# Expert products with the tokens stationary and the weights moving, half rows gathered and scattered, and the down products one expert behind

## The chip, the core and the metric

One core of one Trainium2 chip runs the whole program. The metric is device time in microseconds (us) from launch to end, the median of repeated runs. The core has five engines with a queue each: TensorE (PE; its weight loads are shown apart as PEld), VectorE (DVE), ScalarE (ACT), GpSimd (POOL) and SyncE (SP). Each runs its own list of instructions in order and waits at semaphores for the others. Matrix products read the on-chip memory (SBUF, 128 partitions) and write PSUM, of which each of eight banks holds 128 partitions of 512 floats. DMA engines move data between SBUF and the chip's large memory (HBM).

## The reference

The program is one layer of a decoder over 512 tokens of width 1024: a mixing part (windowed attention, convolution, a matrix memory), then a mixture of experts, then an input embedding. The change is in the mixture. Each token is routed to 2 of 32 experts, so an expert gets 32 tokens in the mean. An expert computes, on its tokens' normed rows:

```
def run_block(args):
    idx, e, w = args
    xb = x_pad[idx]
    hb = jax.nn.silu(xb @ w_gate[e]) * (xb @ w_up[e])
    return (hb @ w_down[e]) * w[:, None]
```

(width 1024 to 256 twice, and back to 1024), and the weighted results are added to the tokens' rows. All of it is in float32.

## The kernel before

**Blocks and table.** An expert has room for BLK = 64 tokens. Tokens beyond 64 would go to overflow blocks, which run only if a count isn't zero; with these inputs none runs. VectorE works out for each of the 1024 (token, choice) pairs its slot, GpSimd scatters 8 x 128 records of four 32-bit words (token, result row, weight, 0) into `table_dram` (L1540), SyncE reads the table back to SBUF with one DMA (L499): slot j in partition j, one column for each block.

**One expert n.** GpSimd gathers its 64 rows of 4 KB from `normed` in HBM into `xr[n % 2]` by an indirect DMA (`gather`, L1557). TensorE turns them, 8 blocks of 64x128, into the bank TR (`turn_block`, L1004), VectorE multiplies by the norm's gain into `xT` (`turned_block`, L1430). `up` (L1013, recorded as L735, the line of the helper `mm`): for each of four 128-wide pieces of the hidden layer (two of gate, two of up) 8 products over the width, with the **weights stationary** (128x128) and the **tokens moving** (64 columns). ScalarE takes the sigmoid (L690), VectorE makes two products (L1438, L1441) that give `hx`, hidden width on partitions. `down` (L1026): four products, tokens stationary (128x64) and 512 columns of the down weights moving. ScalarE scales the low half of the result by the token's weight (L693), VectorE the high half (L1446), into `yr`. GpSimd scatters the 64 rows of 4 KB to `expert_rows` in HBM (`scatter`, L1566).

**What sets the order.** The lists are written by hand. TensorE, for each n: up(n), turn_block(n+1), down(n). GpSimd, for each n: gather(n+2), once block n is turned; then scatter(n), once both halves of expert n's result are scaled. Two small operations (L1549) carry waits ahead of each indirect DMA. SyncE keeps a ring of RING = 4 experts' weights in SBUF (`we`, 3072 KB an expert); the load of expert n+4 (L474) is issued when down(n) is done, and waits for nothing else. After expert 29 and 30 two loads of 2048 KB for the next stage take the place of expert loads (L509).

Ahead of the stage TensorE multiplies the input embedding and ends that before the table is ready. Behind it SyncE reads all of `expert_rows` once the last scatter has landed.

A product of float32 appears in the trace as two records, each a weight load (LDWEIGHTS, PEld) and a pass (MATMUL, PE). "PE bank L735 128*64 128x512" is a pass with 128 rows and 64 columns of weights and 512 moving columns.

## Time and profile before

| | |
|---|---|
| median of 3 runs | 1278.75 us (1278.14 to 1278.79) |
| profiled execution, span of the engines' work | 1272.7 us |
| PE busy | 1173.6 us (92%) |
| PEld busy | 849.9 us (67%) |
| DVE, ACT, POOL busy | 461.0, 288.0, 204.6 us |
| HBM read | 172.06 MB |

The profiled execution has no launch time of its own beside its span; the runs' median is 6.05 us above it, which is what lies around the engines' work. Times in the trace count from the start of the span. The expert stage runs from 801 to 1185 us. A granted clock of 1.00 means that TensorE runs at 2.4 GHz, 0.50 means 1.2 GHz.

### The profile page before, as it was taken

Reading aid. Unit: us, or ns where it says so; the run is one execution under the profiler, and the core shown is the slowest. Engines: PE = TensorE matmul, PEld = TensorE weight load, DVE = VectorE, ACT = ScalarE, POOL = GpSimd, SP = SyncE. Lnnn points to the kernel's source line nnn. Section 1 sums busy time; section 2 is a strip of 40 time slices with the busy share of each in tenths; the row PEclk is TensorE's granted clock in tenths of the full one; section 3 lists DMA queues with packets and bytes.
Section 4 is the critical chain, followed back from the end, with each engine's and each line's share of the span. In section 5 each row is a group of like instructions: output and inputs, shape, how many; then the busy total and the mean of one; then the engine's idle time right before and its main releaser. Section 6 shows DMA issues by size and latency. Waiting matters only on the chain.

```text
span 1272.7 us, 15378 instructions
## 1 busy us (share of the span) xinstructions
PE 1173.6 (92%) x5677; PEld 849.9 (67%) x5677; DVE 461.0 (36%) x981; ACT 288.0 (23%) x449; POOL 204.6 (16%) x384
## 2 busy tenths in 40 slices
PE   6699899899999889999999997799999999999596
PEld 6578678677677656666665464678777877777342
DVE  5594384476457336222321234011111111111433
ACT  2224333433422333111110111010110110110142
POOL 0222401501321110000000002122222222222000
PEclk9899899899899879999999987599999999999798
DMA  4220041031030214221214333178777777774401
GB/s 185 83 83 18 3 146 33 1 132 49 0 115 0 75 74 199 82 75 74 80 68 167 131 139 142 43 294 314 284 275 307 303 275 285 313 289 179 156 17 49
DMA packets 23133, 176.20 MB, mean 138 GB/s; under 512 B 5856, under 2 KB 6336, under 8 KB 16832
## 3 DMA queue, kind: packets, MB, share of 16 engines
q1 hardware_dynamic: 17504, 167.35, 34.4%
q0 software_dynamic: 5600, 8.47, 1.9%
q8 instruction: 18, 0.29, 0.1%
q14 instruction: 11, 0.09, 0.0%
HBM read 172.06 MB, written 12.65 MB: 145 GB/s over the span
## 4 chain that ended last, share of the span: by engine, by line
PE 80%; DVE 8%; issue 6%; DMA 2%; ACT 2%; POOL 1%; DVEq 0%; SPq 0%; ACTq 0%; POOLq 0%
PE bank L735 76%; DVE arena L1199 2%; PE bank L1004 2%; DVE low_parts L1132 2%; DVE arena L1239 1%; DMA arena<-in_w_branch 1%; PE bank L955 1%; PE bank L827 0%; DVE hT_parts L1127 0%; DMA x_sb<-in_x 0%; PE bank L763 0%; POOL table_dram L1540 0%; DMA arena<-expert_rows 0%; ACT arena L605 0%; DMA mT<-normed,gidx 0%
## 5 line engine op out<-in xcount | busy, mean ns | idle before, releaser
L735 PE MATMUL bank<-yT,arena 128*128 128x64 f32 (+1 forms) x2240 | 328.3, 307 | 0.9 <-DVE yT L1430 0.9
L735 PEld LDWEIGHTS bank<-yT,arena 128*128 128x128 f32 x2240 | 274.0, 196 | 63.0 <-issue 60.1
L735 PE MATMUL bank<-arena 128*128 128x64 f32 (+7 forms) x624 | 187.4, 452 | 23.1 <-DVE arena L1223 8.9
L735 PE MATMUL bank<-mT_parts,low_parts 128*128 128x512 f32 x448 | 178.7, 399 | 0.0
L735 PEld LDWEIGHTS bank<-arena 128*128 128x128 f32 (+1 forms) x624 | 108.7, 215 | 97.9 <-issue 70.6
L735 PE MATMUL bank<-mT_parts,x_parts 128*128 128x512 f32 x320 | 139.9, 437 | 17.3 <-DVE low_parts L1132 13.5
L735 PE MATMUL bank<-hT_parts,x_parts 128*128 128x512 f32 x320 | 128.4, 401 | 0.0
L735 PE MATMUL bank<-arena,yT 128*64 128x512 f32 x256 | 118.0, 604 | 0.0
L1132 DVE TENSOR_TENSOR low_parts<-arena,x_parts 128x1024 fp32r<-128x1024 f32 (+1 forms) x44 | 62.3, 1416 | 149.2 <-ACT x_parts L559 117.9
L735 PEld LDWEIGHTS bank<-mT_parts,low_parts 128*128 128x128 f32 x448 | 85.6, 191 | 20.9
L735 PEld LDWEIGHTS bank<-mT_parts,x_parts 128*128 128x128 f32 x320 | 61.8, 193 | 38.8 <-issue 18.8
L1199 DVE SCALAR_TENSOR_TENSOR arena<-arena,chn 128x512 f32<-128x512 f32 x116 | 80.5, 761 | 0.0
L735 PEld LDWEIGHTS bank<-hT_parts,x_parts 128*128 128x128 f32 x320 | 61.9, 193 | 19.0 <-issue 5.7
L735 PE MATMUL bank<-arena,hT 128*128 128x512 f32 (+1 forms) x192 | 72.3, 530 | 0.8 <-DVE hT L1091 0.8
L735 PEld LDWEIGHTS bank<-arena,yT 128*64 128x64 f32 x256 | 32.7, 138 | 59.3 <-issue 57.1
L693 ACT ACTIVATE mT<-bank,table 64x512 f32<-64x512 f32 x32 | 21.8, 682 | 200.8 <-PE bank L735 200.8
L1549 POOL TENSOR_TENSOR takes_wait<-cst 1x1 f32<-1x1 f32 x132 | 24.1, 183 | 264.5 <-issue 253.3
L1239 DVE CUSTOM_DVE_ANT_0 arena<-bank,arena 128x128 f32<-128x128 f32 (+3 forms) x96 | 38.7, 454 | 72.4 <-issue 59.9
L735 PEld LDWEIGHTS bank<-arena,hT 128*128 128x128 f32 x192 | 39.1, 244 | 31.7 <-issue 30.6
L1446 DVE TENSOR_SCALAR mT<-bank,table 64x512 f32<-64x512 f32 x32 | 23.8, 743 | 99.5 <-PE bank L735 99.5
L735 PE MATMUL bank<-mT_parts,cm_high_b 128*128 128x512 f32 x128 | 51.0, 398 | 3.5 <-DVE low_parts L1132 3.5
L1527 POOL TENSOR_TENSOR arena<-arena 128x128 f32<-128x128 f32 (+3 forms) x32 | 31.7, 992 | 124.3 <-ACT arena L605 124.3
(225 smaller groups left out, 1190.1 us busy)
## 6 DMA issues: line engine op xcount, KB each, us to landing
arena<-in_w_expert SPq DMA_DIRECT2D x32, 3072.0 KB, 10.6
arena<-in_w_cm SPq DMA_DIRECT2D x32, 512.0 KB, 3.5
arena<-in_w_gate SPq DMA_DIRECT2D x8, 1536.0 KB, 6.4
arena<-in_w_tm SPq DMA_DIRECT2D x4, 1536.0 KB, 6.8
arena<-in_w_branch SPq DMA_DIRECT2D x8, 768.0 KB, 7.9
x_sb<-in_x SPq DMA_DIRECT2D x8, 512.0 KB, 5.7
arena<-in_w_out SPq DMA_DIRECT2D x1, 4096.0 KB, 12.1
arena<-in_w_pg SPq DMA_DIRECT2D x2, 2048.0 KB, 7.7
```

Source lines behind the costliest of these rows:

```text
L693: act.activation(yr[b2][:, 0:512], OUT[0:BLK, :], ACT.Copy, scale=table_w(col)).then_inc(y_low, 1)
L735: return pe.matmul(out, lhsT, rhs, start=start, stop=stop)
L955: last = pe.transpose((S_16, OUT)[half][:, k * P:(k + 1) * P], x_sb[:, t, (4 * half + k) * P:(4 * half + k + 1) * P], ident)
L1004: last = (pe.matmul if k == 0 else pe.transpose)(TR[:, k * BLK:(k + 1) * BLK], xr[b2][:, k * P:(k + 1) * P], ident[0:BLK, 0:BLK], **(dict( ...
L1132: dve.tensor_tensor(low, weights, high.bitcast(F32), ALU.subtract).then_inc(done, 1)
L1199: dve.scalar_tensor_tensor(cacc[:, j % 2], ypad[:, j:j + SEQ], w31(j), cacc[:, j % 2], ALU.mult, ALU.add).then_inc(conv_step, 1)
L1239: dve.tensor_tensor_reduce(out=sc[:, u % 2, at:at + width], in0=bank[:, 0:width], in1=bias[:, s, b0:b0 + width], scale=1.0, scalar=-3e38, ...
L1446: dve.tensor_scalar(yr[b2][:, 512:1024], S_16[0:BLK, :], table_w(col), None, ALU.mult).then_inc(y_high, 1)
L1527: pool.tensor_tensor(dst[:, 0:n], sc[:, u % 2, 0:n], sc[:, u % 2, n:2 * n], ALU.add).then_inc(pool_step, 1)
L1549: pool.tensor_tensor(takes_wait[:, cell:cell + 1], ones[0:1, 0:1], ones[0:1, 0:1], ALU.add)
```

## The change

Up: the tokens become stationary (128x64) and the weights move. The hidden layer's 512 columns are cut in two sides of 256 (gate piece and up piece of one half); side 0 is multiplied in array columns 0 to 63 with its result in partitions 0 to 63 of a bank, side 1 in array columns 64 to 127 with its result in partitions 64 to 127. Down does the same with two sides of 512 columns in one bank. The hidden block now has tokens on partitions, so TensorE turns it (one 128x128) and ScalarE copies it back. The rows are gathered and scattered as 128 half rows of 2 KB; the table holds a record for each half. TensorE's list puts down(n) behind up(n+1). Banks for up (GU), down (Y) and the small tiles are doubled.

```
-        xr = [mflat[0:BLK, b * D:(b + 1) * D] for b in range(2)]
-        yr = [mflat[0:BLK, (2 + b) * D:(3 + b) * D] for b in range(2)]
+        xr = [mflat[:, b * 512:(b + 1) * 512] for b in range(2)]
+        yr = [mflat[:, (2 + b) * 512:(3 + b) * 512] for b in range(2)]
+        normed_halves = normed.rearrange("s (h c) -> (s h) c", h=2)
+        expert_halves = expert_rows.rearrange("s (h c) -> (s h) c", h=2)
+        GU, HT, Y = (MM, S_1), S_4, (OUT, S_16)
...
-            sp.dma_start(table[:, :, :], table_dram.rearrange("(j b) w -> j b w", b=NBLK)).then_inc(table_loaded, 16)
+            for half in range(2):
+                sp.dma_start(table[half * BLK:(half + 1) * BLK, :, :],
+                             table_dram.rearrange("(j b) w -> j b w", b=NBLK)[:, :, 4 * half:4 * half + 4])\
+                  .then_inc(table_loaded, 16)
...
-            def expert(n, b2, col, first_wait):
-
-                act.wait_ge(g_done, n + 1)
-                act.activation(sgx, MM[:, 0:2 * BLK], ACT.Sigmoid).then_inc(gate_sig, 1)
-                act.wait_ge(down_done, 2 * n + 1)
-                first_wait()
-                act.activation(yr[b2][:, 0:512], OUT[0:BLK, :], ACT.Copy,
-                               scale=table_w(col)).then_inc(y_low, 1)
+            def hidden_copy(n, b2):
+
+                act.wait_ge(h_turned, n + 1)
+                act.activation(hx[b2], HT[:, 0:P].rearrange("p (j s) -> p j s", j=2), ACT.Copy).then_inc(hx_ready, 1)
+
+            def scale_rows(n, b2, scattered):
+
+                act.wait_ge(down_done, n + 1)
+                act.wait_ge(rows_scattered[b2], scattered)
+                act.activation(yr[b2], Y[b2][:, :], ACT.Copy, scale=table_w(n)).then_inc(y_scaled, 1)
...
+                for k in range(KD // 2):
+                    last = pe.transpose(TR[:, k * P:(k + 1) * P], xr[b2][:, k * P:(k + 1) * P], ident)
+                last.then_inc(rows_turned, 1)
+
+            def up(n, b2, w, gu_free):
+
+                pe.wait_ge(xT_ready, n + 1)
+                gu_free()
                 for k in range(KD):
-
-                    last = (pe.matmul if k == 0 else pe.transpose)(
-                        TR[:, k * BLK:(k + 1) * BLK], xr[b2][:, k * P:(k + 1) * P], ident[0:BLK, 0:BLK],
-                        **(dict(start=True, stop=True) if k == 0 else {}))
-                last.then_inc(rows_turned, 1)
-
-            def up(n, b2, w):
-
-                for m in range(4):
-                    for k in range(KD):
-                        last = mm((MM, S_1)[m // 2][:, m % 2 * BLK:(m % 2 + 1) * BLK],
-                                  w[:, k * 512 + m * P:k * 512 + (m + 1) * P],
-                                  xT[b2][:, k, :], k == 0, k == KD - 1)
-                    if m % 2:
-                        last.then_inc((g_done, u_done)[m // 2], 1)
-
-            def down(n, w):
+                    for side in range(2):
+                        last = mm(GU[b2][side * BLK:(side + 1) * BLK, 0:2 * P], xT[b2][:, k % 4, k // 4, :],
+                                  w[:, k * 512 + side * 2 * P:k * 512 + (side + 1) * 2 * P], k == 0, k == KD - 1)
+                last.then_inc(up_done, 1)
+
+            def turn_hidden(n, b2):
+
+                pe.wait_ge(h_swished, n + 1)
+                pe.transpose(HT[:, 0:P], hs[b2], ident).then_inc(h_turned, 1)
+
+            def down(n, b2, w, y_free):
+
                 pe.wait_ge(hx_ready, n + 1)
-                pe.wait_ge(y_low, FREE + n)
-                pe.wait_ge(y_high, FREE + n)
-                for half in range(2):
-                    for j in range(2):
-                        at = 4096 + j * 1024 + half * 512
-                        last = mm((OUT, S_16)[half][0:BLK, :], hx[:, j, :], w[:, at:at + 512], j == 0, j == 1)
-                    last.then_inc(down_done, 1)
+                y_free()
+                for j in range(2):
+                    for side in range(2):
+                        at = 4096 + j * 1024 + side * 512
+                        last = mm(Y[b2][side * BLK:(side + 1) * BLK, :], hx[b2][:, j, :], w[:, at:at + 512], j == 0, j == 1)
+                last.then_inc(down_done, 1)
...
+            def expert_step(n, i, b, first=False, y_unused=False, last_one=False, before_last=False):
+                b2, other = b % 2, (b + 1) % 2
+                if not last_one:
+                    pe.wait_ge(we_loaded[(b + 1) % RING], (i + 1 + (b + 1) // RING) * 16)
+                    up(n + 1, other, we[(b + 1) % RING],
+                       nothing if first else lambda: pe.wait_ge(h_swished, n))
+                turn_hidden(n, b2)
+                if not last_one and not before_last:
+                    turn_block(n + 2, b2, rows_gathered[b2], (2 * i + (b + 2) // 2 + 1) * 16)
+                down(n, b2, we[b], nothing if y_unused else lambda: pe.wait_ge(y_scaled, n - 1))
...
-            dve.tensor_copy(info[:, :, 0], const("token"))
-            dve.tensor_copy(info[:, :, 1], const("row"))
-            dve.memset(info[:, :, 3], 0)
-            dve.tensor_copy(info[:, :, 2].bitcast(F32), flat(6)).then_inc(routed, 1)
+            for half in range(2):
+                ours = slice(half * 2 * T, (half + 1) * 2 * T)
+                dve.tensor_copy(info[:, :, 4 * half], const("token")[:, ours])
+                dve.tensor_copy(info[:, :, 4 * half + 1], const("row")[:, ours])
+                dve.memset(info[:, :, 4 * half + 3], 0)
+                last = dve.tensor_copy(info[:, :, 4 * half + 2].bitcast(F32), flat(6))
+            last.then_inc(routed, 1)
...
+            def serve(n, b2, gathers, scattered):
+
+                if gathers is not None:
+                    pool.wait_ge(rows_turned, n + 1)
+                    pool.wait_ge(rows_gathered[b2], gathers)
+                    gather(b2, n + 2, rows_gathered[b2], 2 + 2 * n)
+                pool.wait_ge(y_scaled, n + 1)
+                pool.wait_ge(rows_scattered[b2], scattered)
+                scatter(b2, n, rows_scattered[b2], NEXP + n if gathers is None else 3 + 2 * n)
```

On TensorE, one expert of the loop in the order of before (`yT` holds the tokens xT and hidden tiles, `arena` the weights, `mT` the gathered rows, `cst` the identity; x31 means 31 more of the row above):

```order
L735 MATMUL bank<-yT,arena 128x64 [waits xT_ready]
L735 MATMUL bank<-yT,arena 128x64 x31
L1004 MATMUL bank<-cst,mT 128x64 [waits xT_ready,rows_gathered1]
L1004 MATMUL bank<-cst,mT 128x64 x7
L735 MATMUL bank<-arena,yT 64x512 [waits y_high,y_low,hx_ready]
L735 MATMUL bank<-arena,yT 64x512 x3
```

And the same place of the change, from one up to the next:

```order
L759 MATMUL bank<-arena,yT 64x256 [waits h_swished,xT_ready]
L759 MATMUL bank<-arena,yT 64x256 x15
L1044 MATMUL bank<-cst,yT 128x128 [waits h_swished]
L1028 MATMUL bank<-cst,mT 128x128 [waits xT_ready,rows_gathered1]
L1028 MATMUL bank<-cst,mT 128x128 x3
L759 MATMUL bank<-arena,yT 64x512 [waits y_scaled,hx_ready]
L759 MATMUL bank<-arena,yT 64x512 x3
```

The four pieces stand in the same order, but they belong to other experts: before, up(n), the turn of n+1, down(n); now, up(n+1), the turn of the hidden block n, the turn of rows n+2, down(n).

On GpSimd, from one scatter's wait to the next gather, before (`gidx` and `sidx` are the indices taken from the table):

```order
L1549 TENSOR_TENSOR takes_wait<-cst 1x1 [waits rows_scattered0,y_high,y_low]
L1563 COPY sidx<-table 64x2
L1564 REGISTER_ALU
L1549 TENSOR_TENSOR takes_wait<-cst 1x1 [waits idx_copied]
L1566 DMA expert_rows<-mT,sidx 1024x1024
L1549 TENSOR_TENSOR takes_wait<-cst 1x1 [waits rows_gathered1,rows_turned]
L1554 ISA
L1554 COPY gidx<-table 64x2
L1555 ISA
L1549 TENSOR_TENSOR takes_wait<-cst 1x1 [waits idx_copied]
L1557 DMA mT<-normed,gidx 64x1024
```

And now:

```order
L1589 TENSOR_TENSOR takes_wait<-cst 1x1 [waits rows_scattered0,y_scaled]
L1603 COPY sidx<-table 128x2
L1604 REGISTER_ALU
L1589 TENSOR_TENSOR takes_wait<-cst 1x1 [waits idx_copied]
L1606 DMA expert_rows<-mT,sidx 2048x512
L1589 TENSOR_TENSOR takes_wait<-cst 1x1 [waits rows_gathered1,rows_turned]
L1594 ISA
L1594 COPY gidx<-table 128x2
L1595 ISA
L1589 TENSOR_TENSOR takes_wait<-cst 1x1 [waits idx_copied]
L1597 DMA mT<-normed,gidx 128x512
```

Nothing moved on GpSimd: scatter(n-1) still stands ahead of gather(n+2), with the same waits, one semaphore (`y_scaled`) where there were two.

## Rows read from the trace of the kernel before

**Rows 1.** The page, chain that ended last: shares of the span by line.
```profile
PE bank L735 76%; DVE arena L1199 2%; PE bank L1004 2%; DVE low_parts L1132 2%; DVE arena L1239 1%; DMA arena<-in_w_branch 1%; PE bank L955 1%; PE bank L827 0%; DVE hT_parts L1127 0%; DMA x_sb<-in_x 0%; PE bank L763 0%; POOL table_dram L1540 0%; DMA arena<-expert_rows 0%; ACT arena L605 0%; DMA mT<-normed,gidx 0%
```
**Rows 2.** Windows: stretch and length, busy by engine (PE, PEld, DVE, ACT, POOL), clock, DMA share, GB/s.
```profile
835.01:846.68 11.67, 11.67 (x82) 8.97 (x81) 2.02 (x4) 0.96 (x2) 2.88 (x8) 1.00 0.75 290
```
**Rows 3.** Timeline of one expert: start, length, engine, line, operation, [idle before].
```profile
831.44 3.65 PE L735 MATMUL bank<-arena,yT 128*64 128x512 f32 x8
...
832.35 0.14 PEld L735 LDWEIGHTS bank<-arena,yT 128*64 128x64 f32 x1 [0.29 <-issue]
...
833.52 0.68 ACT L693 ACTIVATE mT<-bank,table 64x512 f32<-64x512 f32 x1 [6.07 <-PE bank L735]
...
835.01 7.36 PE L735 MATMUL bank<-yT,arena 128*128 128x64 f32 x64
835.26 0.74 DVE L1446 TENSOR_SCALAR mT<-bank,table 64x512 f32<-64x512 f32 x1 [3.02 <-PE bank L735]
...
837.25 0.94 POOL L1566 DMA_INDIRECT expert_rows<-mT,sidx  x1 [0.55 <-issue]
...
839.29 0.97 POOL L1557 DMA_INDIRECT mT<-normed,gidx  x1 [0.52 <-issue]
...
853.97 0.87 PE L1004 MATMUL bank<-cst,mT 64*128 64x64 f32 x9
```
**Rows 4.** Load and gather of that expert: issue in the timeline, then size and us to landing.
```profile
835.27 0.34 SPq L474 DMA_DIRECT2D arena<-in_w_expert  x1
...
arena<-in_w_expert SPq DMA_DIRECT2D x1, 3072.0 KB, 10.5
...
mT<-normed,gidx POOLq DMA_INDIRECT x1, 6.8
```
**Rows 5.** All 34 gathers, from issue to landing; then the pair at 1150 to 1155 us.
```profile
DMA to landing us min/median/max: 2.0/6.9/7.8
...
1150.11 0.34 SPq L509 DMA_DIRECT2D arena<-in_w_pg  x1
...
arena<-in_w_pg SPq DMA_DIRECT2D x1, 2048.0 KB, 7.8
...
1154.40 0.97 POOL L1557 DMA_INDIRECT mT<-normed,gidx  x1 [0.52 <-issue]
...
mT<-normed,gidx POOLq DMA_INDIRECT x1, 3.9
```
**Rows 6.** Windows around pauses of TensorE; the clock is the third number from the end.
```profile
791.40:793.70 2.30, 0.00 (x0) 0.00 (x0) 0.00 (x0) 1.08 (x2) 1.31 (x2) 1.00 0.03 2
793.80:801.00 7.20, 0.00 (x0) 0.00 (x0) 0.00 (x0) 1.28 (x1) 2.98 (x8) 0.50 0.12 31
...
1198.10:1206.70 8.60, 7.81 (x15) 4.07 (x16) 7.24 (x7) 3.30 (x6) 0.00 (x0) 0.50 0.53 213
...
60.20:63.30 3.10, 3.08 (x7) 2.48 (x8) 2.81 (x4) 0.00 (x0) 2.95 (x4) 0.50 0.00 0
63.40:70.00 6.60, 6.60 (x30) 5.36 (x29) 6.60 (x8) 2.51 (x3) 6.60 (x5) 1.00 0.18 53
```
**Rows 7.** Timeline at the lower clock: the first down products, and eight turns of 128x128.
```profile
818.53 4.89 PE L735 MATMUL bank<-arena,yT 128*64 128x512 f32 x8
...
819.43 0.23 PEld L735 LDWEIGHTS bank<-arena,yT 128*64 128x64 f32 x1 [0.62 <-issue]
...
1198.11 1.94 PE L955 MATMUL bank<-cst,x_sb 128*128 128x128 f32 x8 [13.03 <-DVE x_sb L1471]
```
**Rows 8.** Ahead of the stage: writes of the table, its reading, and the chain's first gather.
```profile
L1540 POOL DMA_INDIRECT table_dram<-info,where x8: 971/972/1103, 782.9 to 792.0; - x8
...
table<-table_dram SPq DMA_DIRECT2D x1, 48.0 KB, 2.1
...
797.44 3.49 DMA mT<-normed,gidx
801.06 1.42 PE bank L1004 x9
```

More of the change, by code:

```diff
@@ L115, in constants @@
     k, t = np.divmod(np.arange(2 * T), T)
-    put("token", t[None] * P + row)
-    put("row", k[None] * SEQ + t[None] * P + row)
+    for name, whole in (("token", t[None] * P + row), ("row", k[None] * SEQ + t[None] * P + row)):
+        put(name, np.concatenate([2 * whole, 2 * whole + 1], 1))
     return c
@@ L1029, in _, with nothing @@
+            def nothing():
+                pass
             pe.wait_ge(ple_copied, 2 * T)
-            pe.wait_ge(table_loaded, 16)
+            pe.wait_ge(table_loaded, 32)
             turn_block(0, 0, rows_gathered[0], 16, first=True)
@@ L1492, in _ @@
         def _(pool):
-            pool.memset(table[:, :, :], OUT_OF_RANGE).then_inc(ready, 1)
+            pool.memset(blank[:, :, :], 2 * OUT_OF_RANGE).then_inc(ready, 1)
             pool.wait_ge(ready, 1)
@@ L1496, in _ @@
                 slots = slice(half * BLK // 2, (half + 1) * BLK // 2)
-                pool.dma_start(table_dram.rearrange("(j b) w -> j b w", b=NBLK)[slots], table[slots, :, :])\
+                pool.dma_start(table_dram.rearrange("(j b) w -> j b w", b=NBLK)[slots], blank[slots, :, :])\
                     .then_inc(rows_scattered[half], 16)
+            for half in range(2):
+                pool.wait_ge(rows_scattered[half], 16)
             pool.wait_ge(if_projected, T)
@@ L1534, in _ @@
             pool.wait_ge(x2_mm, 2 * T)
-            pool.memset(mflat[0:BLK, 0:2 * D], 0.0).then_inc(ready, 1)
-            for half in range(2):
-                pool.wait_ge(rows_scattered[half], 16)
+            pool.memset(mflat[:, 0:D], 0.0).then_inc(ready, 1)
             pool.wait_ge(routed, 1)
```

162 lines of the change are left out of this document (83 added, 79 removed).

## Prediction

> **What bounds the kernel now.** I read the chain of work that ended last first: 76% of the span stands on the one line of TensorE's products, L735 [rows 1]. Then the windows. In the expert stage TensorE is busy for 11.67 of the 11.67 us of an expert, at the full clock (1.00, 2.4 GHz), while the DMA engines are 0.75 busy [rows 2]. So one expert costs 11.67 us of TensorE, and 32 of them the stretch from 803 to 1185 us.
>
> The timeline of one step says what those 11.67 us are [rows 3]: 64 records of a weight load of 128 columns with 64 moving columns (7.36 us; each product is two records), a turn of the next rows (0.87 us), and 8 records of 512 columns (3.65 us). The first group is paced by its weight loads, 7.36 / 64 = 0.115 us each. The last is paced by its columns: 0.14 + 0.29 = 0.43 us a record [rows 3].
>
> The question for this change is what else runs at the period of a step and is hidden now. Call D the end of an expert's down product; in rows 3 it is 831.44 + 3.65 = 835.09. From D on: VectorE scales the high half until 836.00, GpSimd issues the scatter at 837.25 and then the gather at 839.29 [rows 3]. SyncE issues the next load of 3072 KB at 835.27 and it lands 10.5 us later, at 845.8 [rows 4]. The gather lands 6.8 us after its issue, at 846.09, that is **D + 11.0 us** [rows 3, 4]. Its rows are turned only at 853.97 [rows 3], so 7.9 us of slack hide it.
>
> That 6.8 us is no outlier: over 34 gathers the median is 6.9 us, the least 2.0 [rows 5]. What makes it long is the load in flight. With no load the first gathers take about 3.5 us [rows 8] and the quickest 2.0; with the 2048 KB load that is issued at 1150.11 and lands at 1157.9, the gather issued at 1154.40 lands at 1158.3 [rows 5]. A gather that is issued behind a load lands together with the load's end or a few tenths later, in both sizes of load.
>
> **The change, part by part.**
>
> *Up products.* 32 products become 16, thus 64 records become 32 of 256 columns with 64-column weights. A record of 512 columns takes 0.43 us, so one of 256 takes about 0.21. Without overlap of the two column tiles that is 32 x 0.215 = 6.9 us, against 7.36. No row shows two column tiles, so overlap is bounded: none, or each tile's record beside its neighbour's. The two records of one product share a tile and can't overlap each other, which leaves 17 slots of 32, 3.7 us. I take the overlap: the two tiles share neither weights nor output partitions, and the trace already has weight loads (PEld) running inside matmuls. At the lower clock a slot is twice as long (0.23 + 0.62 = 0.85 us for 512 columns [rows 7]): 7.2 us.
>
> *Down products.* Still 8 records of 512 columns: 3.65 us without overlap, 5 slots of 8 with it, 5 x 0.43 + 0.2 = 2.35 us; at the lower clock 7.05 and 4.5 us.
>
> *Turns.* Nine records of 64 rows become four of 128x128, and one more turns the hidden block. Eight such take 1.94 us at the lower clock [rows 7]: four are 0.97 us there and about half, 0.5, at the full one; a single one is 0.24 or 0.12.
>
> *Down one expert behind.* This hides what waits between up and down: sigmoid, two products on VectorE, the copy on ScalarE. It also moves the turn. Before, in step n TensorE does up(n), turn(n+1), down(n). After, it does up(n+1), turn of the hidden block, turn(n+2), down(n). GpSimd's order is as before: gather(n+2) stands behind scatter(n-1), which waits for the scaled rows of expert n-1, so for D(n-1). So the gather that is issued after D(n-1) is now wanted in the very next step, ahead of down(n), instead of one step later. The 7.9 us of slack are gone, and behind the waiting turn on TensorE stand down(n) and all that follows; behind down(n) stand SyncE's next load, the scaling, the scatter and the next gather. **The loop closes on itself**: D(n) = D(n-1) + gather's landing + turn + down. Up, however fast, lies inside the wait.
>
> *Halved rows.* One DMA carries 128 half rows instead of 64 rows, the same bytes. GpSimd's indirect DMAs of 128 pieces take 0.97 us [rows 8], those of 64 rows 0.94 to 0.97 [rows 3]: nothing. ScalarE scales 64x512 in 0.68 us and VectorE did its half in 0.74 [rows 3]; one 128x512 scale takes the place of both, so the gather is issued at D + 4.2 as before. The load is issued at D as before. So I keep D + 11.0 for the landing, with 9.8 as lower bound (the moved bytes lie on more partitions, so the gather may get through before the load is done) and 11.3 above.
>
> *The clock.* TensorE will now stand idle each period, for about 11.1 us less the up products. Where TensorE's work ended at 791.4, the trace shows the granted clock at 1.00 for 2.3 us more and at 0.50 from 793.8; where work began again at 60.2 the clock was back after 3.2 us, and where it began at 1198.1 it was still at 0.50 after 8.6 us [rows 6]. With up at 3.7 to 7.2 us the idle time is 4 to 7 us, so turn and down meet the lower clock (1.2 GHz).
>
> *The period* at the lower clock: 11.0 + 0.14 (from landing to the first turn, 797.44 + 3.49 to 801.06 [rows 8]) + 0.97 + 4.5 = 16.6 us. At the full clock 11.0 + 0.14 + 0.5 + 2.35 = 14.0. I take **16.0**: nearer the first, less what an early landing or a clock that rises within down gives.
>
> *Ends of the stage.* Steps 1 to 29 wait for such a gather: 29 x (16.0 - 11.67) = +125.6 us. The start (turn, up(0), up(1), turn, down(0), mostly at the lower clock: 0.97 + 0.85 + 7.3 + 0.97 + 0.85 + 5.5 + 0.25 + 0.6 + 3.0 = 20.3) against 818.53 + 4.89 - 801.06 = 22.4 [rows 7, 8]: -2. Steps 30 and 31 have no turn of rows: about 13 us against 23.3, -10.4.
>
> *The table.* It is written as before, with four more VectorE operations ahead (about +0.3 us), and read by two DMAs of 16-byte pieces, 3,072 each, where one of 64 long rows took 2.1 us [rows 8]. TensorE, idle since 791.4, waits for it in full. Below: one more issue, +0.5. Above I allow +8; I take +3.
>
> The Trainium skill, "DMA: Bandwidth & Descriptors", on rules for authors, says that a last dimension that isn't contiguous becomes one descriptor per element. It gives no time for 16-byte runs, and no row here does.
>
> Sum against the profiled execution (span 1272.7, about 6 us less than its launches of 1278.75; that difference stays): 125.6 - 2 - 10.4 + 3.3 = **+116.5 us, 1395 us**.
>
> **Rivals.**
>
> *Loop as forecast, products overlapping, lower clock: chance 0.52.* 1395; with a landing from 9.8 to 11.3 us and the clock somewhere within turn and down, periods of 15 to 16.9 us, 1366 to 1421.
>
> *Loop, overlap, full clock: 0.12.* Period 14.0: 29 x 2.33 = 67.6, 1337. For it: in the expert stage now the clock holds at 1.00 with few columns a record. Against: the falls of rows 6.
>
> *Loop, no overlap: 0.20.* Up takes 6.9 to 13.7 us, down 3.65 to 7.05; the period is 15.3 at the full clock and 19.2 at the lower, but TensorE then stands idle 4 us at most, so mixed, some 17.3: 29 x 5.6 = 163, with ends +5 and -7 and the table: 1443 (1390 to 1500).
>
> *The gather takes turns with the load: 0.08.* It lands at some D + 9, and with overlap the period is 14.3: about 1345. The Trainium skill, "DMA: Bandwidth & Descriptors", Queues, rings and completion order, says that each engine goes round between queues packet by packet. In this trace the gathers nevertheless land with the load's end, at 6.8 us, so as yet the rule doesn't bring one out early.
>
> *The other side, faster: 0.06.* If the gather lands as without a load, 2.0 to 3.5 us after its issue at D + 4.2, so at D + 7.7 at most, the period is 7.7 + 0.14 + 0.5 + 2.35 = 10.7 us: 29 x 1.0 = 29 us less, with the ends 1240. It turns at a landing of D + 8.7 with the full clock. Against it stand the gathers beside loads, at 6.9 us in the median [rows 5].
>
> *Nothing changes: 0.02*, the accident of a period of 11.67.
>
> **How the numbers follow.** The range leaves out the faster case, the same and most of the no-overlap case above 1450, and takes in the full clock: 1335 to 1450. About 0.2% (2.6 us) is what a measurement of this kernel tells from no change: slower 0.92, same 0.02, faster 0.06.
>
> **What would show it.** In the profile after: ahead of each 128x128 turn of rows TensorE idle for 4 us or more, released by the gather's DMA; gather to landing near 7 us; one load in flight, issued at down's end; granted clock well below 1.00 in the stage; DMA share about 0.55; four turns, then down, then up. Overlap shows in the spacing of the 256-column records, 0.11 us in the mean against 0.21. I am wrong if TensorE doesn't wait for the gather: then the period is 11 us or less, and what ends the wait is a load or nothing. I am wrong in size if the landing isn't D + 11.0.

## The result

| | before | after |
|---|---|---|
| launches | 1278.45 us, median of 4 (1274.82 to 1278.79) | 1367.99 us, median of 4 (1366.5 to 1368.64) |
| profiled span | 1272.7 us | 1364.7 us |

The ratio is 1.0706 (95% interval 1.0691 to 1.0721): slower by 7.1%, 89.5 us between the medians, 92.0 us between the spans. The launch whose profile gave the span of 1364.7 us took 1366.5 us, so 1.8 us lie around a span. One launch of run 9 below, of 1981.6 us, stands far outside all others and is left out of every comparison.

### The profile page after: what moved, and what is told of

The parts are those of the page before. It is cut to its first block, busy times and chain, and to the rows that moved or that the text cites. A ratio compares the mean times of both kernels' runs of the same rounds, so it can differ in the third digit from the quotient of the medians.

```text
span 1364.7 us, 12866 instructions
## 1 busy us (share of the span) xinstructions
PE 1057.2 (77%) x4516; PEld 686.4 (50%) x4516; DVE 437.7 (32%) x952; ACT 286.9 (21%) x474; POOL 206.7 (15%) x376
## 4 chain that ended last, share of the span: by engine, by line
PE 48%; issue 32%; DVE 7%; POOL 6%; DMA 3%; ACT 2%; POOLq 1%; DVEq 0%; SPq 0%; ACTq 0%
PE bank L759 47%; POOL mT L1597 2%; DVE arena L1243 2%; POOL takes_wait L1589 2%; DVE low_parts L1176 1%; DMA mT<-normed,gidx 1%; DVE arena L1283 1%; POOL expert_rows L1606 1%; DMA arena<-in_w_branch 1%; PE bank L979 1%; PE bank L851 0%; DVE hT_parts L1171 0%; PE bank L787 0%; DMA x_sb<-in_x 0%; POOL table_dram L1580 0%
## 5 line engine op out<-in xcount | busy, mean ns | idle before, releaser
L759 PE MATMUL bank<-arena,yT 128*64 128x256 f32 (+1 forms) x1280 | 223.1, 511 | 3.1 <-DVE yT L1477 2.1
L759 PE MATMUL bank<-arena 128*128 128x64 f32 (+7 forms) x624 | 190.8, 460 | 23.3 <-DVE arena L1267 8.9
L1028 PE MATMUL bank<-cst,mT 128*128 128x128 f32 x128 | 34.7, 424 | 217.5 <-DMA mT<-normed,gidx 217.5
L759 PE MATMUL bank<-mT_parts,low_parts 128*128 128x512 f32 x448 | 178.0, 397 | 0.0
L759 PEld LDWEIGHTS bank<-arena,yT 128*64 128x64 f32 x1280 | 102.6, 161 | 118.1 <-issue 86.0
L759 PEld LDWEIGHTS bank<-arena 128*128 128x128 f32 (+1 forms) x624 | 111.9, 222 | 98.5 <-issue 70.9
L759 PE MATMUL bank<-mT_parts,x_parts 128*128 128x512 f32 x320 | 138.3, 432 | 17.1 <-DVE low_parts L1176 13.3
L1028 PEld LDWEIGHTS bank<-cst,mT 128*128 128x128 f32 x128 | 22.3, 212 | 224.1 <-DMA mT<-normed,gidx 208.9
L759 PE MATMUL bank<-hT_parts,x_parts 128*128 128x512 f32 x320 | 128.4, 401 | 0.0
L1477 DVE TENSOR_TENSOR yT<-bank,chn 128x512 f32<-128x512 f32 x32 | 22.1, 691 | 237.5 <-PE bank L1028 237.5
L759 PEld LDWEIGHTS bank<-mT_parts,low_parts 128*128 128x128 f32 x448 | 85.0, 190 | 20.0
L709 ACT ACTIVATE mT<-bank,table 128x512 f32<-128x512 f32 x32 | 22.0, 687 | 334.3 <-PE bank L759 334.3
L759 PE MATMUL bank<-yT,arena 128*128 128x512 f32 x192 | 86.3, 592 | 0.0
L759 PEld LDWEIGHTS bank<-mT_parts,x_parts 128*128 128x128 f32 x320 | 61.2, 191 | 39.3 <-issue 18.8
L1484 DVE TENSOR_TENSOR yT<-bank,yT 128x128 f32<-128x128 f32 x32 | 9.3, 292 | 206.9 <-ACT yT L698 206.9
L759 PE MATMUL bank<-arena,hT 128*128 128x512 f32 (+1 forms) x192 | 71.2, 524 | 0.8 <-DVE hT L1135 0.8
L759 PEld LDWEIGHTS bank<-hT_parts,x_parts 128*128 128x128 f32 x320 | 61.3, 192 | 18.9 <-issue 5.7
L759 PEld LDWEIGHTS bank<-yT,arena 128*128 128x128 f32 x192 | 36.3, 189 | 37.1 <-issue 35.0
## 6 DMA issues: line engine op xcount, KB each, us to landing
arena<-in_w_expert SPq DMA_DIRECT2D x32, 3072.0 KB, 10.4
```

What stands on the lines that cost most here:

```text
L709: act.activation(yr[b2], Y[b2][:, :], ACT.Copy, scale=table_w(n)).then_inc(y_scaled, 1)
L759: return pe.matmul(out, lhsT, rhs, start=start, stop=stop)
L1028: last = pe.transpose(TR[:, k * P:(k + 1) * P], xr[b2][:, k * P:(k + 1) * P], ident)
L1477: dve.tensor_tensor(xT[b2], TR[:, :].rearrange("p (k h s) -> p k h s", k=KD // 2, h=2), chn[:, G_FFN:G_FFN + KD].rearrange("p (h k) -> p k ...
L1484: dve.tensor_tensor(sgx[b2], GU[b2][:, 0:P], sgx[b2], ALU.mult).then_inc(gate_mul, 1)
```

## The profile after

The page first: busy time of TensorE with its share and its instructions, the clock in 40 slices, the costliest groups (last field: idle time before them and who ended it), and the chain of work that ended last, by line. The new names: L759 is `mm`, L1028 the turn of rows, L1044 the turn of the hidden block, L709 the scaling, L1597 the gather, L1606 the scatter.

```profile
PE 1057.2 (77%) x4516; PEld 686.4 (50%) x4516; DVE 437.7 (32%) x952; ACT 286.9 (21%) x474; POOL 206.7 (15%) x376
...
PEclk9899899899899799999999578777777777777798
...
PE bank L759 47%; POOL mT L1597 2%; DVE arena L1243 2%; POOL takes_wait L1589 2%; DVE low_parts L1176 1%; DMA mT<-normed,gidx 1%; DVE arena L1283 1%; POOL expert_rows L1606 1%; DMA arena<-in_w_branch 1%; PE bank L979 1%; PE bank L851 0%; DVE hT_parts L1171 0%; PE bank L787 0%; DMA x_sb<-in_x 0%; POOL table_dram L1580 0%
...
L1028 PE MATMUL bank<-cst,mT 128*128 128x128 f32 x128 | 34.7, 424 | 217.5 <-DMA mT<-normed,gidx 217.5
```

TensorE does 116 us less work than before (1173.6), and the kernel is longer. Its share of the chain falls from 76% [rows 1] to 47%, and the last row says where the time went: ahead of the turns of rows TensorE sat idle for 217.5 us, and all of it ended with the landing of a gather.

The windows show 300 us of the stage, and then one half-clock and one full-clock stretch of a single period (columns as in [rows 2]):

```profile
860.00:1160.00 300.00, 159.16 (x866) 77.41 (x862) 24.82 (x59) 23.51 (x59) 59.88 (x157) 0.72 0.57 225
...
986.99:993.82 6.83, 3.42 (x10) 1.49 (x12) 0.69 (x1) 0.00 (x0) 0.00 (x0) 0.50 0.34 141
994.00:1000.50 6.50, 4.25 (x37) 2.33 (x33) 0.58 (x2) 1.21 (x3) 3.06 (x8) 1.00 0.78 284
```

Against [rows 2], TensorE is busy for 53% of the time instead of all of it, the clock is 0.72 instead of 1.00, the DMA engines 0.57 instead of 0.75. Nothing is a bound by its load. The timeline of one period, and how long the gathers took from issue to landing (least, median, most), show the loop:

```profile
990.40 1.11 PE L1028 MATMUL bank<-cst,mT 128*128 128x128 f32 x4 [6.76 <-DMA mT<-normed,gidx]
991.45 6.55 PE L759 MATMUL bank<-arena,yT 128*64 128x512 f32 x40
...
994.71 0.69 ACT L709 ACTIVATE mT<-bank,table 128x512 f32<-128x512 f32 x1 [10.75 <-PE bank L759]
994.73 0.33 SPq L479 DMA_DIRECT2D arena<-in_w_expert  x1
...
996.60 1.01 POOL L1606 DMA_INDIRECT expert_rows<-mT,sidx  x1 [0.55 <-issue]
...
997.93 0.33 PE L1044 MATMUL bank<-cst,yT 128*128 128x128 f32 x1
...
998.74 1.07 POOL L1597 DMA_INDIRECT mT<-normed,gidx  x1 [0.52 <-issue]
1005.50 0.90 PE L1028 MATMUL bank<-cst,mT 128*128 128x128 f32 x3 [7.25 <-DMA mT<-normed,gidx]
...
DMA to landing us min/median/max: 2.9/6.7/7.4
```

Down and up are merged in one row of 40 records. Down ends at D = 994.5, where the scaling and the load start (994.71, 994.73). The gather is issued at D + 4.2, its rows are turned at D + 11.0, and 7.25 us of that TensorE waits. From 990.40 to 1005.50 are 15.1 us; over 28 periods, by the starts of the scalings, the mean is 15.40 us (14.7 to 16.5), against 11.67 before. The mean period is made of 10.99 us from D to the turn of rows, 1.04 for the turn and 3.36 for down.

The up products, first at the lower and then at the full clock:

```profile
810.56 6.50 PE L759 MATMUL bank<-arena,yT 128*64 128x256 f32 x32 [0.94 <-DVE yT L1477]
...
818.77 3.67 PE L759 MATMUL bank<-arena,yT 128*64 128x256 f32 x32 [1.12 <-DVE yT L1477]
```

3.67 us for 32 records is 0.115 us a record: the two column tiles do overlap. And the reading of the table, now two DMAs:

```profile
798.31 2.42 SPq L505 DMA_DIRECT2D table<-table_dram  x2
803.92 0.18 POOL L1589 TENSOR_TENSOR takes_wait<-cst 1x1 f32<-1x1 f32 x1 [6.76 <-DMA table<-table_dram]
```

From issue to GpSimd's first operation behind it are 5.6 us, where before the DMA took 2.1 [rows 8].

## The experiments

Theory: the loop as forecast, D(n) = D(n-1) + landing + turn + down, closed by the place of the turn ahead of down, with a landing set by the load that is in flight. Rivals: the tiling or the half rows cost the time; the products don't overlap; the lower clock comes from elsewhere and is the cause.

A ratio is to the kernel before as launched beside the run (medians 1276.24 us for runs 1 to 4, 1277.32 for 5 to 8, 1278.38 for 9 and 10); a difference to after is to its 1367.99 us. Runs 3, 4 and 5 are one launch each, so their times carry no interval, and what is read from them is read in their traces. "..." in a cut of code stands for changed lines that aren't shown.

**1. Gathers one expert further ahead.** GpSimd gathers n+3 where it gathered n+2; TensorE's order stays.

```
-                    pool.wait_ge(rows_turned, n + 1)
-                    pool.wait_ge(rows_gathered[b2], gathers)
-                    gather(b2, n + 2, rows_gathered[b2], 2 + 2 * n)
+                    pool.wait_ge(rows_turned, n + 2)
+                    pool.wait_ge(rows_gathered[1 - b2], gathers)
+                    gather(1 - b2, n + 3, rows_gathered[1 - b2], 3 + 2 * n)
...
```

> The changed kernel with GpSimd's gathers one expert further ahead: gather(n+3) in place of gather(n+2) stands between scatter(n-1) and scatter(n), in the same two buffers; all products and their order are kept. Loop theory (each step waits for a gather that is issued 4.2 us after the down product before it and lands with the weight load in flight): the wait of 7 us ahead of each turn goes, the next bound is the weight load at about 8.5 to 10 us a step, time 1180 to 1215 us. Clock rival (the time is lost because TensorE works at 1.2 GHz): its work at that clock is about 13 us a step, so 1290 to 1310 us. Load rival (a load or the halved rows bound the period): no change, 1360 to 1370 us.

Measured: 1211.15 us, ratio to before 0.9495 (0.9464 to 0.9525), 157 us less than after. Waits of TensorE from 860 to 1160 us (in total, times, longest), and the DMAs of that stretch:

```profile
PE bank L1028 <- DMA mT<-normed,gidx: 68.7, 13, 7.1
...
mT<-normed,gidx POOLq DMA_INDIRECT x24, 8.7
```

What follows: the gather's issue behind down(n-1) is the loop. Broken, half of the waits are gone (13 in some 28 steps, where after has one in each); most periods alternate, about 6 and 14 us. Two loads are queued then, a load takes 12.3 us in the median where after's takes 10.4, and the gathers take 8.7 us. The time is in the range expected, but the theory had the wait gone, and it is still there in every second step.

**2. TensorE's old order, all else as after.** up(n), turn(n+1), turn of the hidden block, down(n).

```
-                    up(n + 1, other, we[(b + 1) % RING],
-                       nothing if first else lambda: pe.wait_ge(h_swished, n))
+                up(n, b2, we[b], nothing if first else lambda: pe.wait_ge(h_swished, n))
+                if not last_one:
+                    turn_block(n + 1, other, rows_gathered[other], (2 * i + (b + 1) // 2 + 1) * 16)
                 turn_hidden(n, b2)
-                if not last_one and not before_last:
-                    turn_block(n + 2, b2, rows_gathered[b2], (2 * i + (b + 2) // 2 + 1) * 16)
...
```

> The changed kernel with TensorE's order of before: up(n), turn of rows n+1, turn of hidden n, down(n), and ScalarE's list to match; tokens stationary, two column tiles and half rows kept; GpSimd untouched. Loop theory: the gather has a step of slack again, so the period is the larger of TensorE's work with its two short waits for the hidden block (3.4 + 0.6 + 1.3 + 0.1 + 0.5 + 1.9 = 7.8 us at the full clock, about 13 at the lower) and of the load (8.5 to 10 us): 1185 to 1225 us. Load rival: about 1365 us. Clock rival: above 1290 us.

Measured: 1199.86 us, ratio 0.9399 (0.9359 to 0.944). The new order alone costs 168 us on top of the new tiles. Periods are 7.0, 7.3 and 14.8 us in turn; what is left of the wait:

```profile
PE bank L1026 <- DMA mT<-normed,gidx: 50.7, 14, 6.5
```

**3. Loads of 384 columns instead of 6144.** The products of experts 4 to 31 then use old weights in the other columns.

```
-                    expert_weights(b, RING * (i + 1) + b)
+                    sp.dma_start(we[b][:, 0:384], w_expert[RING * (i + 1) + b, :, 0:384]).then_inc(we_loaded[b], 16)
```

> The changed kernel, but the 28 weight loads inside the expert loop bring only 384 of 6144 columns (192 KB in place of 3072), so experts 4 to 31 compute with old weights for the rest. Loop theory with the landing set by the load: gathers land about 3 us after issue instead of 6.7, the period is 4.2 + 3.0 + 0.15 + 0.8 + 2.5 = 10.7 us, time about 1230 us. Rival (the landing is long because 128 half rows take long): gathers stay near 6.7 us and the period near 15.3, 1360 us.

Measured: 1256.34 us. The gathers of 860 to 1160 us, from issue to landing in the median:

```profile
mT<-normed,gidx POOLq DMA_INDIRECT x26, 2.9
...
903.58 0.33 SPq L513 DMA_DIRECT2D arena<-in_w_expert  x1
...
907.58 1.07 POOL L1597 DMA_INDIRECT mT<-normed,gidx  x1 [0.53 <-issue]
910.93 1.12 PE L1028 MATMUL bank<-cst,mT 128*128 128x128 f32 x4 [3.42 <-DMA mT<-normed,gidx]
```

With 192 KB in place of 3072 the landing is 3.8 us earlier, and D + 7.5, turn 1.1 and down 3.1 give a period of 11.7 us (mean 11.6), 3.8 less than after. The loop is still there: TensorE waits 3.42 us in this step. The period is 0.9 us longer than expected, and the time 26 us, because down still met the lower clock: 3.4 us in the mean, where the expectation had 2.5.

**4. The sides one after the other.** In up and down the loop over the side stands outside.

```
-                for k in range(KD):
-                    for side in range(2):
+                for side in range(2):
+                    for k in range(KD):
```

> The changed kernel with the products of one side of a result all ahead of those of the other, in up and in down, so that neighbouring records stand in the same column tile; same number of products, same results. If the two tiles overlap now: down takes 8 slots instead of 4, 3.6 us at the full and 7 at the lower clock against 1.9 and 3.4, up 7 to 13.7 us which lies inside the wait for the gather; period up by 1.5 to 3 us, time 1410 to 1460 us. Rival (no overlap in the changed kernel): within 5 us of 1368.

Measured: 1372.94 us, 5 more than after and so below the 1410 to 1460 that I expected if the tiles overlap; by the time alone the rival would fit. The timeline of one period shows why it doesn't:

```profile
1011.98 1.12 PE L1028 MATMUL bank<-cst,mT 128*128 128x128 f32 x4 [4.70 <-DMA mT<-normed,gidx]
1013.03 10.28 PE L759 MATMUL bank<-arena,yT 128*64 128x512 f32 x40
1016.93 15.61 SPq L479 DMA_DIRECT2D arena<-in_w_expert  x2
1021.00 1.07 POOL L1597 DMA_INDIRECT mT<-normed,gidx  x1 [0.53 <-issue]
1023.23 0.33 PE L1044 MATMUL bank<-cst,yT 128*128 128x128 f32 x1
1027.91 1.11 PE L1028 MATMUL bank<-cst,mT 128*128 128x128 f32 x4 [4.35 <-DMA mT<-normed,gidx]
```

Down and up take 10.28 us instead of 6.55, and TensorE waits 4.35 us instead of 7.25: nearly all that up takes longer comes out of the wait. Up's speed is worth nothing in this loop: the mean period is 15.45 us against 15.40, and the 5 us lie ahead of the first scaling (830.32 us against 825.27), where up is not hidden. The starts of the weight loads, first of up and then of down, both at the lower clock, tell where the overlap went (x1: one load every 0.23 + 0.20 us, for 256 columns; x2: a pair every 0.24 + 0.61 us, for 512):

```profile
985.87 0.23 PEld L759 LDWEIGHTS bank<-arena,yT 128*64 128x64 f32 x1 [0.20 <-issue]
...
998.42 0.24 PEld L759 LDWEIGHTS bank<-arena,yT 128*64 128x64 f32 x2 [0.61 <-issue]
```

Up runs record by record now, down still in pairs, 3.3 to 3.7 us in all, so this run shows the lost overlap for up alone. That down would lose it too was my mistake in the expectation; what the loop costs without overlap in down no run shows.

**5. TensorE kept busy in the wait.** Seven products more in each step.

```
                 if not last_one and not before_last:
+                    for _ in range(7):
+                        mm(PA[:, :], ident, cst[:, 0:512])
```

> The kernel after, with seven products of 512 columns more (14 records, about 6.0 us at the full clock) on TensorE in each step, between the turn of the hidden block and the turn of the rows; they write a bank that nothing reads, and fill the time in which TensorE waits for the gather. Theory (the gather sets the period from D + 10.8 us on, and the lower clock stretches what stands behind it): the granted clock in the stage rises to 0.95 or more, the turn takes 0.60 us instead of 1.10 and the down product 1.7 to 1.9 us instead of 3.1, the period is 10.8 + 0.15 + 0.6 + 1.9 = 13.45 us instead of 15.37, and the time 1368 - 30 x 1.9 = about 1310 us, although TensorE has 6 us more to do in each step. Rival (the clock falls for another reason than the idle time, or the time is TensorE's own work): the clock stays near 0.73 and the 14 records, now 12 us, come on top of the path: 1400 us or more.

Measured: 1318.51 us, 49.5 less than after, with 30 x 14 records of 0.43 us, 180 us of useless work, on TensorE (its busy time grows by 120, since the rest runs faster). Windows, then the turn and the down product of one period:

```profile
860.00:1100.00 240.00, 218.43 (x1048) 104.04 (x1046) 22.95 (x54) 21.18 (x53) 54.48 (x142) 1.00 0.65 255
...
963.73 0.66 PE L1028 MATMUL bank<-cst,mT 128*128 128x128 f32 x4 [1.45 <-DMA mT<-normed,gidx]
...
964.31 1.94 PE L759 MATMUL bank<-arena,yT 128*64 128x512 f32 x8
```

The clock is 1.00, turn and down take 0.66 and 1.94 us, the period is 13.4 (forecast for this run: 13.45). So the idle time brings the lower clock, and the lower clock is 2.0 of the 3.7 us by which a period is longer than before: 0.46 in the turn, 1.42 in down, and 0.1 in an earlier turn. The loop alone is the rest. Of the 8 us above the 1310 expected, 6.7 lie ahead of the first scaling (831.97 us against 825.27).

**6. The kernel before, with the new order alone.** Its tiles, 64 full rows a gather, its table; two buffers for the hidden block.

```
+                    pe.wait_ge(hx_ready, n + 1)
+                    up(n + 1, (b + 1) % 2, we[(b + 1) % RING])
+                    turn_block(n + 2, b % 2, rows_gathered[b % 2], (2 * i + (b + 2) // 2 + 1) * 16)
+                down(n, b % 2, we[b])
...
```

> The kernel before with one part of the change alone: the down product of expert n stands behind up(n+1) and turn(n+2), the hidden block having two buffers; products, 64 full rows a gather and the table are those of before. Theory (the order alone closes the loop through the gather, and the tiling has no part in it): TensorE waits 2.5 to 5 us for the gather in each step, the period is 11.0 + 0.15 + 0.9 + 3.65 = 15.7 us at the full clock and up to 18 where the lower one catches turn and down: 29 x 4.0 to 6.3, so 1395 to 1455 us, I say 1410. Rival (the half rows, the wider gathers or the column tiles are what costs): the order costs nothing or helps a little, 1270 to 1285 us.

Measured: 1470.49 us, ratio 1.1523 (1.1485 to 1.1561), and so above the range that I gave it. TensorE's timeline:

```profile
953.57 7.36 PE L745 MATMUL bank<-yT,arena 128*128 128x64 f32 x64
964.73 1.43 PE L1014 MATMUL bank<-cst,mT 64*128 64x64 f32 x9 [3.80 <-DMA mT<-normed,gidx]
966.09 5.46 PE L745 MATMUL bank<-arena,yT 128*64 128x512 f32 x8
971.48 7.36 PE L745 MATMUL bank<-yT,arena 128*128 128x64 f32 x64
983.17 1.11 PE L1014 MATMUL bank<-cst,mT 64*128 64x64 f32 x6 [4.33 <-DMA mT<-normed,gidx]
```

Here D is 953.5 and 971.5: the next turn comes at D + 11.2 and D + 11.7, turn and down take 6.8 us because most of both meets the lower clock (mean 0.82), the period is 18.15 us in the mean: 28 x 6.5 = 182 us. What my range left out is the start of the stage: the first scaling begins at 840.58 us and not at 821.95, 18.6 later: two up products of 13.9 us each now stand ahead of it, at a clock of 0.50 all the while. (The two make 200 us, the difference of the spans; the launch that was profiled, 1475.14 us, is the slowest of the four.) The order alone makes the kernel before slower by 15%; tiles and half rows have no part in the loss. The two orders and the two tilings together:

| | old order | new order |
|---|---|---|
| old tiles, full rows | 1278 | 1470 |
| new tiles, half rows | 1200 | 1368 |

In the old order the new tiles, half rows and doubled banks together gain 78 us.

**7. Old order, gathers four experts ahead**, in four buffers.

```
-                    gather(b2, n + 2, rows_gathered[b2], 2 + 2 * n)
+                    gather(b4, n + 4, rows_gathered[b4], 4 + 2 * n)
...
```

> The kernel after with TensorE's old order (up(n), turn(n+1), hidden turn, down(n)), and with the gathers four experts ahead, in four buffers with a semaphore each, where the old order alone took 1199.9 us and still waited for a gather in every second step. Theory (what is left there is the gather that lands late behind two queued loads, and once it is gone the loads bound the step): no wait for gathers in the stage, DMA share 0.93 or more, the period 8.5 to 9.1 us where 3072 KB and the rows take about 8 to 8.5 us of the DMA engines: 1199.9 - 30 x 0.6 to 1.1 = 1165 to 1182 us. Rival (the period is set by something else than the gather's lead, for example TensorE's chain up, sigmoid, products, turn, down, or the scatters): the wait moves to another releaser and the time stays at 1195 to 1203 us.

Measured: 1154.95 us, ratio 0.9047 (0.9013 to 0.9081). In the stretch from 860 to 1100 us no wait of TensorE names a gather, and the windows say

```profile
860.00:1100.00 240.00, 190.07 (x1177) 97.25 (x1176) 43.90 (x96) 46.06 (x95) 74.14 (x194) 0.90 0.89 371
```

The DMA engines are 0.89 busy, where I expected 0.93 or more. Fifteen of the 31 periods lie at 8.9 to 9.6 us, the others at 6.3 to 7.5. The time is 10 us below the lower end of what I expected, since not all steps are held by the loads. In the short ones the trace shows TensorE's own chain: in the period from 926.26 to 933.37 us it is busy for 5.39, 0.66 and 0.33 us (down and up, turn of rows, turn of the hidden block) and idle only for 0.44 and 0.37 us, for the hidden block.

**8. The same, with the table of before**, read twice in long rows; GpSimd adds one to the upper half's numbers.

```
-                             table_dram.rearrange("(j b) w -> j b w", b=NBLK)[:, :, 4 * half:4 * half + 4])\
+                             table_dram.rearrange("(j b) w -> j b w", b=NBLK))\
...
+            pool.tensor_scalar(table[BLK:P, :, 0:2], table[BLK:P, :, 0:2], 1, None, ALU.add).then_inc(ready, 1)
```

> The run with four gathers ahead once more, and the table of four words as before: it is read twice in long rows of 768 bytes, once for each half of the partitions, and GpSimd adds one to the upper half's row numbers, instead of two reads of 3,072 pieces of 16 bytes. Theory (the pieces cost the 3.5 us by which the read is longer after than before, 5.6 against 2.1 us): the read takes 2.2 to 2.6 us, GpSimd's addition 0.2 to 0.5 us more, so 2.5 to 3.5 us less than the run with four gathers. Rival (the table's read overlaps the wait for the first gather or the first expert's load, so the pieces cost nothing): within 1 us of it.

Measured: 1150.56 us, ratio 0.9014 (0.8979 to 0.9049): 4.4 us less than run 7, but the intervals overlap, so the profile has to say it:

```profile
794.77 1.16 SPq L505 DMA_DIRECT2D table<-table_dram  x2
797.55 0.48 POOL L1577 TENSOR_SCALAR table<-table 64x96 int32<-64x96 int32 x1 [3.92 <-DMA table<-table_dram]
```

From issue to GpSimd 2.8 us, where run 7 has 5.75, less 0.5 for the addition: the pieces of 16 bytes cost 2.5 us net. The rest of the 4.4 can't be told from the differences between launches. This is the fastest version here, 9.9% faster than before.

**9. The load held back until the gather has landed.** The kernel after, one wait more on SyncE.

```
                     sp.wait_ge(down_done, RING * i + b + 1)
+                    sp.wait_ge(rows_gathered[(b + 1) % 2], (2 * i + (b + 3) // 2 + 1) * 16)
                     expert_weights(b, RING * (i + 1) + b)
```

> The kernel after with one wait more: SyncE issues the load that follows down(n) only when the gather that follows down(n) has landed. TensorE's order and its wait for the gather stay. Theory (the gather takes 6.7 us because the load issued at D is in flight, 2.9 us where it isn't): the gather lands 2.9 us after its issue, at D + 7.1, while the load now runs from there for 8 to 10 us and reaches 15 to 18 us past D, into the next period's gather; so the period lies between 7.1 + 0.15 + 1.1 + 3.1 = 11.5 us and, where the load's tail holds the next gather up by 1 to 2 us, 13.5: 1368 - 30 x 1.9 to 3.9 = 1251 to 1311, I say 1275 us. Rival (what counts is that a load of 3072 KB goes through once a period, whenever it is issued, or the scatter just ahead of the gather holds it up): the landing stays near 6.7 us and the time at 1360 to 1375.

Measured: 1264.07, 1260.88 and 1258.68 us, ratio 0.9854 (0.9834 to 0.9875): 107 us less than after, by an additional wait. DMAs of 860 to 1160 us with their median time to landing, and two turns:

```profile
arena<-in_w_expert SPq DMA_DIRECT2D x25, 3072.0 KB, 10.1
...
mT<-normed,gidx POOLq DMA_INDIRECT x26, 3.1
...
961.80 0.65 PE L1029 MATMUL bank<-cst,mT 128*128 128x128 f32 x4 [2.92 <-DMA mT<-normed,gidx]
...
972.97 1.11 PE L1029 MATMUL bank<-cst,mT 128*128 128x128 f32 x4 [3.25 <-DMA mT<-normed,gidx]
```

The same 3072 KB go through once a period, and the gather lands after 3.1 us instead of 6.7. So it is the load that was issued before the gather that holds it up, not the load as such; and the scatter just ahead, which is there in both, doesn't do it alone. The period is 11.7 us, like that of run 3, near the lower end of what was expected: the load's tail holds the next gather up hardly at all.

**10. The turn behind down.** The kernel after, one call moved.

```
                 turn_hidden(n, b2)
+                down(n, b2, we[b], nothing if y_unused else lambda: pe.wait_ge(y_scaled, n - 1))
                 if not last_one and not before_last:
                     turn_block(n + 2, b2, rows_gathered[b2], (2 * i + (b + 2) // 2 + 1) * 16)
-                down(n, b2, we[b], nothing if y_unused else lambda: pe.wait_ge(y_scaled, n - 1))
```

> The kernel after with one thing moved on TensorE: the turn of rows n+2 stands behind down(n) instead of ahead of it; the down products stay one expert behind, GpSimd's and SyncE's order stay. Theory (what closes the loop is the turn ahead of down: down(n) waits for the gather that follows down(n-1)): with the turn behind, that gather holds up only up(n+2) and so down(n+1), thus two steps share 11 + 0.6 to 1.1 for the turn, 0.7 for the copy, 3.7 to 6.5 for up, 0.3 and 1.9 to 3.1 for down, 18.2 to 22.7 us, a period of 9.1 to 11.4 us: 1368 - 30 x 4.0 to 6.3 = 1180 to 1250 us, I say 1205. Rival (a down product that is one expert behind frees the weights and the block too late wherever the turn stands): TensorE waits for the gather once in every step and the time stays above 1340 us.

Measured: 1220.39 us, ratio 0.9532 (0.9504 to 0.9561). Waits of 860 to 1160 us, and two steps:

```profile
PE bank L1028 <- DMA mT<-normed,gidx: 45.2, 13, 8.3
...
953.38 0.66 PE L1028 MATMUL bank<-cst,mT 128*128 128x128 f32 x4
...
964.33 0.66 PE L1028 MATMUL bank<-cst,mT 128*128 128x128 f32 x4 [3.27 <-DMA mT<-normed,gidx]
```

Down is still one expert behind, and 148 us of time are gone. One step in two waits; periods are 7.5 and some 13 us. That the down product lags is harmless; the turn ahead of it closes the loop.

## Why the prediction was right, step by step

**The loop: right.** The wait stands where it was put, ahead of each turn of rows, 30 times, released by the gather. Runs 1, 2 and 10 each open it at another place (issue, order of up and down, place of the turn) and gain 148 to 168 us; run 6 builds it into the kernel before and loses 193.

**The landing at D + 11.0: right** (D + 4.2 and 6.7 to 6.8 us), and so was its cause, the load in flight, by runs 3 and 9. That the scatter ahead of the gather has a part in it (run 9) I hadn't seen.

**The lower clock: right in kind.** Mean 0.72, turns at 1.09 to 1.11 us against 0.97 forecast. Run 5 prices it at 2.0 us a period; the forecast had 16.6 less 14.0, 2.6.

**Overlap of the column tiles: right; its size in down wrong.** Of the period's 0.6 us of error (15.4 for 16.0) this is the step that failed: "5 slots of 8" for down. The 8 records run in 4 pairs. Down takes 3.68 us where it meets the lower clock throughout, in 14 of 28 periods, and 2.85 to 3.5 where the clock rises within it (3.1 in the period shown, 994.54 less 991.45); the mean is 3.36, where the forecast had 4.5. So 16.6 less 0.8 for the fourth slot, 0.3 for the clock and 0.1 for a shorter way from landing to turn is 15.4; I had taken off 0.6 for an early landing and the clock. I had the second record of a product wait for its first and the other tile start one slot later. The records of the two tiles start together (7 ns apart, at 991.448 and 991.455). In run 4 four records of one side stand ahead of the other side's, and the pairs are there still, 14 ns apart, while in up, with 16 a side, only the last four records of the first side run beside the first four of the second (from 1019.63 us). Both fit a second tile that can start four records ahead of its turn; other depths weren't tried.

The Trainium skill, "TensorEngine Tiling (Array Packing)", Key Properties, says that different tiles can run weight loads and matmuls in parallel. The trace agrees: 3.67 us for the 32 records of up, where run 4 needs 6.8.

**The sum.** By the scalings' starts the stage is 361.6 us before and 453.5 after, +91.9: 28 periods of 15.40 for 11.67 are +104.4, the last three intervals (12.9, 6.6, 2.9) -12.5. The forecast had 29 x 4.33 = +125.6 and -10.4. So 28 x 0.6 = 17 us are the period, 3 the 29th one, which was already short, 3 the last two steps.

The start of the stage, from the first turn to the first scaling, was -4.2. The forecast's -2 went to the end of the first down product; measured so, it is 16.5 us for 22.4, -5.9, because up(1) and down(0) ran at the full clock (3.67 and 1.94 us, forecast 5.5 and 3.0).

The table was +4.5 for +3.3: +3.5 for the read (forecast 3) and +1.0 from the routing's first turn to the table's first write (35.5 us, before 34.4). The forecast had 0.3 there for VectorE's four more operations, and they took 0.1: from VectorE's first write of the records to the table's first write are 1.44 us, before 1.30. The other 0.9 lie in the router's 64 products, 12.75 us for 11.83, which the change doesn't touch; why they are longer is open.

3.1 us more were there before any instruction that the change touches (before's own launches differ by 4), and 3.2 fewer lie behind the last scaling, 1.6 of them because ScalarE before scaled its half while down was still running. In all 91.9 - 4.2 + 4.5 + 3.1 - 3.2 = 92.1, and the spans differ by 92.0.

**What lies around the span: wrong**, 1.8 us (2.5 in later runs of the kernel before) and not 6, because I set the span of one execution against the median of others.

**The rivals.** No overlap: refuted by up's 3.67 us. What it would have cost no run shows. The 48 us that I gave it (1443 for 1395) rest in the main on down, 7.05 us for 4.5 in the period; run 4 took the overlap from up alone, which costs 5 us, and down kept its pairs. Full clock: run 5 is that case, 1318.5 where 1337 was forecast. Gather in turns with the load: its time is refuted, the gather lands with the load. The Trainium skill, "DMA: Bandwidth & Descriptors", Queues, rings and completion order, has the engines go round by packet, and in the same section says that a DMA's semaphore write lands only after every earlier write of that engine, across its queues. The trace agrees with the first: GpSimd's packets and the load's take turns in rounds of 1.07 us (run 9), but these turns go to the scatter. The second isn't what makes the 6.7 us: the row packets themselves run late, and from the last of them to the landing are 0.5 us in after, in run 3 and in run 9 alike.

## What to carry to other kernels

When an operation is moved past another on the engine that bounds, follow each of its inputs back to its issue: if the issue waits in order behind the result that the moved operation now stands in front of, the latency that a step of slack had hidden becomes the period. Then speed on that engine buys nothing, and its idle time takes the clock down as well. A small transfer that is on such a path should be issued ahead of the large one, or the large one held back for it: here that single wait was worth 107 us.

## What was unexpected of the hardware

- A gather of 128 half rows behind a load of 3072 KB lands 6.7 us after its issue, ahead of it after 3.1, and the load takes 10.1 to 10.4 us either way. The gather moves only the slots that hold a token: the 52 gathers and scatters of run 9 from 860 to 1160 us moved 6.70 MB, 0.13 MB each.
- Two column tiles overlap fully also with the two records of a float32 product: 8 records of 512 columns in 1.94 us at the full clock, 3.65 without tiles [rows 3]. With four records a side the order of the sides didn't matter, with 16 it did.
- 180 us of useless products made the kernel 49.5 us faster, by the clock (one launch).
- 6,144 pieces of 16 bytes took 5.6 to 5.8 us where 128 rows of 768 bytes took 2.8.
